# Two blocks on one core: the rotary rotation of the first two projections taken from TensorE and given to VectorE as four signed 32-row multiplications

## Chip, core and metric

One core of one Trainium2 chip runs the whole program as one launch. The metric is the device time in microseconds of that core, lower is better. The engines are named PE (TensorE), DVE (VectorE), ACT (ScalarE), POOL (GpSimd) and SP (SyncE, which issues DMAs).

## What is computed

The program is two layers of a first transformer (a sparse attention called NSA, then a dilated attention) and one layer of a second, on 512 tokens of width 1024. Each layer projects its normed input, turns queries and keys by a rotary embedding and attends. Only the rotary step matters here:

```python
def rope(x):
    T = x.shape[1]
    half = x.shape[-1] // 2
...
    x1, x2 = xf[..., :half], xf[..., half:]
    return jnp.concatenate([x1 * cos - x2 * sin, x2 * cos + x1 * sin], axis=-1).astype(x.dtype)
```

A head has 64 dimensions, so x1 and x2 are halves of 32. In the kernel a projected unit holds two heads on 128 rows (partitions), 512 tokens along a row: x1 and x2 of each head are quarters of 32 rows, and the rotation swaps neighbouring quarters and changes the sign of one.

## The kernel before

**A projection unit.** A projection is made in units of 128 output features by 512 tokens, each in one of four PSUM banks (unit u in bank u % 4). The weights of a unit are one piece of 512 KB. SP loads pieces into a ring of four slots (`ask_pieces`, L221). ACT copies the piece into a high part (`split_hi`, L232) and POOL subtracts to get the low part (`split_lo`, L240); three split pieces can be held. PE then makes 24 products of 128x512 for the unit (`feature_unit`, L264): 8 slices of the width by high-high, high-low, low-high. The first two or three units of a phase are interleaved in `feature_group` (L276).

**The rotary step** of unit r is `rope_parts`, in four instructions after ACT has copied the unit from PSUM to SBUF (L878 in the first projection, L1398 in the dilated one):
- PE multiplies the SBUF copy by a constant 128x128 matrix `rot` that swaps the quarters with sign, into bank 4 + r % 2 (L710, an fp32 product);
- POOL multiplies the SBUF copy by the cosine table into `t1` (L716);
- DVE multiplies the rotated PSUM bank by the sine table into `t2` in SBUF (L722);
- DVE adds `t1` and `t2` (L725), with both inputs in SBUF.

`t1` and `t2` have two buffers each, so the step of r waits for the sum of r-2 (semaphore `rope_roped`).

**First projection (NSA).** 23 units: two of the compression's input (u 0 and 1), ten that are turned (u 2 to 11, rotary r = u - 2), three pieces of the values (u 12 to 14), eight of the gate z. On PE, written out by hand: the units up to 11, the product of rotary step u - 4 behind unit u (r 0 to 7 so); then the compression's first layer, 8 unsplit pieces against taps of its input (L802, 64 matmuls, banks 6 and 7); then the products of r 8 and 9; then the values, where for each slice of the width four token tiles (i 0 to 3) are accumulated in banks 0 to 3 (`token_unit`, L305, 96 matmuls). The values' banks are those of units 8 to 11, so each tile first waits until ACT has evacuated that unit (`left2`). ACT's order is `split_hi` of u + 2, then the copy of u; its split of piece 12 stands ahead of its copy of unit 10. POOL's order is cosine of r 7, split of 12, cosine of r 8, split of 13, cosine of r 9, split of 14.

**Dilated projection.** 32 units (8 queries, 8 keys, 8 values, 8 z), of which 16 are turned: PE makes the product of r = u - 2 behind unit u, u 2 to 17. Values are transposed on PE behind units 17 to 24. ACT copies unit r into `raw6`, four buffers, and waits for the sum of r - 4.

The second transformer has five rotary steps of its own (`rope_two`), which use `rope_parts` with another table.

Of the kernel before, what the change touches and what calls it, by code (L numbers as in the profile page):

```python
# [24 lines left out]
ALU = mybir.AluOpType  # L25
# [3 lines left out]
P = 128  # L29
T = 512  # L30
# [4 lines left out]
HALF = DH // 2  # L35
# [67 lines left out]
V_COLS = 2 * P + 3 * NH  # L103
# [5 lines left out]
def build(nc, w_stream, consts_in, small_dram, x_in, pos_in, perm_in, u_in, v_in, u_rows, out, gates_dram, gelu_dram):  # L109
    ctx = ExitStack()  # L110
    with ctx:
# [3 lines left out]
        def sem(name):  # L115
            return ctx.enter_context(nc.semaphore(name))
# [32 lines left out]
        def C(name):  # L149
            a, b = CONST_AT[name]  # L150
            return cst[:, a:b]
# [191 lines left out]
        h_parts = (h_hi, h_lo)  # L343
# [356 lines left out]
        def rope_parts(tag, n, raw, t1, t2, dst, cos, sin, bank0, raw_ready):  # L700
# [25 lines left out]

            return pe_part, pool_part, dve_part, roped, sined

        def evacuated(order, sems):

            def wait(eng, i):
                sems[order[i]].wait(eng, sum(o == order[i] for o in order[:i + 1]))
            return wait
# [19 lines left out]
        ev2 = {who: since("evacuated_" + who, order2.count(who)) for who in ("dve", "act")}  # L753
        left2 = evacuated(order2, ev2)
        h1_sum, h1_done, cmp_sum, cmp_zero = sem("h1_sum"), sem("h1_done"), sem("cmp_sum"), sem("cmp_zero")
        rope_nsa = rope_parts("r0", 10, lambda r: rp[:, r, :], rt1, rt2, lambda r: qr[:, r, :],
                              C("cos"), C("sin"), 4, lambda eng, r: left2(eng, r + 2))
        sc = area(WORK, 2, NH * CMP_PAD)
        pc = area(WORK + 1272, 2, NH * CMP_PAD)
        ptc = area(WORK + 2296, 4 * P)  # L760
# [12 lines left out]
        with phase() as block:  # L773
# [5 lines left out]
            def _(pe):  # L779
                def free(u):  # L780
                    if u >= 4:
                        left2(pe, u - 4)

                feature_group(pe, units2[0:2], (0, 1), h_parts, n0.done)
                for u in range(2, 12):
                    free(u)
                    feature_unit(pe, piece_of(u), u % 4, h_parts)
                    if u >= 4:
                        rope_nsa[0](pe, u - 4)

                for kv in range(2):
                    if kv == 0:
                        left2(pe, 1)
                    for q4 in range(4):
                        w = piece_ready(pe, PIECES["cmp_w1"][kv * 4 + q4])
                        for m in range(4):
# [5 lines left out]
                                mm = pe.matmul(o, wt, x[:, kv, :, tap:tap + 8 * (N_CMP - 1) + 1:8],  # L802
                                               start=(tap == 0), stop=(tap == 15))
                        mm.then_inc(piece_used, 1)
                rope_nsa[0](pe, 8)
                rope_nsa[0](pe, 9)
                token_unit(pe, PIECES["vsw"], 0, V_COLS, 3, h_parts, tile_tokens,
                           lambda pe, i: left2(pe, 8 + i))
                pe.wait_ge(h1_done, 2)
                for g in range(2):  # L810
                    for ch in range(2):
# [37 lines left out]

                for u in range(15, 23):  # L850
                    if u < 17:
                        rope_nsa[4].wait(pe, u - 6)
                    else:
                        left2(pe, u - 2)
                    if u == 22:
                        pe.wait_ge(c_sub, TT)
                        ada_chunk(pe, 2, ada_sum2, 0)
                    feature_unit(pe, piece_of(u), 4 + (u - 15) % 2, h_parts)
                    if u == 16:
                        cmp_scores(0)  # L860
                        cmp_scores(1)
                        cmp_scores(2)
                    elif u == 17:
                        cmp_turn(0)
                        cmp_scores(3)
                    elif 18 <= u < 21:
                        cmp_turn(u - 17)
                        cmp_values(u - 18)
                    elif u == 21:
                        cmp_values(3)  # L870
# [437 lines left out]
        with phase() as block:  # L1308
# [19 lines left out]
            def act5(act):  # L1328
                for u in range(KD):
# [9 lines left out]
        vd = area(12288, TT, D)  # L1339
        od = area(16384, TT, D)  # L1340
        raw6 = area(16384, 4, T)
        rt61, rt62 = area(18432, 2, T), area(19456, 2, T)
        vt6 = area(20480, 2, T)
        v_turned, v_taken = sem("v_turned"), sem("v_taken")
        order6 = ["act"] * 32
        ev6 = {who: since("evacuated_" + who, order6.count(who)) for who in ("dve", "act")}
        left6 = evacuated(order6, ev6)
        rope_dil = rope_parts("r6", 16, lambda r: raw6[:, r % 4, :], rt61, rt62,
                              lambda r: (qd if r < 8 else kd)[:, r % 8, :], C("cos"), C("sin"), 4, left6)
        units6 = [n for name in ("dq", "dk", "dv", "dz") for n in PIECES[name]]  # L1350
        orders_in = sem("orders_in")
        orders = area(23552, 2 * P + 2 * TT + TT * NH)
        to_tile, to_class = orders[:, 0:P], orders[:, P:2 * P]
# [2 lines left out]
        with phase() as block:  # L1356
# [5 lines left out]
            @block.tensor  # L1362
            def _(pe):
                n1.pe_spread(pe)
                feature_group(pe, units6[0:3], (0, 1, 2), h_parts, n1.done)
                for u in range(2, 32):
                    if u >= 4:
                        left6(pe, u - 4)
                    if u >= 3:
                        feature_unit(pe, units6[u], u % 4, h_parts)  # L1370
                    if 2 <= u < 18:
                        rope_dil[0](pe, u - 2)
                    if 17 <= u < 25:
                        v = u - 17
                        left6(pe, u - 1)
                        if v >= 2:
                            pe.wait_ge(v_taken, v - 1)
                        for i in range(TT):
                            mm = pe.transpose(ps[:, 6 + v % 2, i * P:(i + 1) * P],
                                              vt6[:, v % 2, i * P:(i + 1) * P], ident)  # L1380
                        mm.then_inc(v_turned, 1)
# [1106 lines left out]
def constants():  # L2488
# [3 lines left out]
    def put(name, a):  # L2492
        lo, hi = CONST_AT[name]
        c[:, lo:hi] = a.reshape(P, hi - lo)
# [13 lines left out]
    inv = inv.astype(np.float32)[p % HALF]  # L2508
    angle = (np.arange(T, dtype=np.float32)[None, :] * inv[:, None]).astype(np.float64)
    put("cos", np.cos(angle))  # L2510
    put("sin", np.sin(angle))
    u = np.arange(T)
    put("causal", np.where(u[None, :] - (T - P) <= p[:, None], 0.0, -BIG))
    d = p[:, None] - p[None, :]
# [117 lines left out]
```

## Time and profile before

| | us |
|---|---|
| median of 3 runs | 2369.14 |
| lowest and highest of them | 2362.18, 2375.37 |
| the profiled execution, its time | 2366.45 |
| its span, first to last instruction | 2364.7 |
| PE busy in the span | 2251.7 |
| DVE, ACT, POOL busy | 1519.5, 917.4, 1313.3 |
| mean granted clock of PE | 0.975 of 2.4 GHz |

A trace is one execution. Time on it is counted from the first instruction. The first projection runs from about 52 to 220 us, the attention of NSA after it to about 445, the dilated projection from 508 to 703. A "wait" is the idle time of an engine ahead of an instruction and what ended it. "PEclk" is the clock that PE was granted: 1.00 is 2.4 GHz, 0.50 is 1.2 GHz. PE's durations overlap: the pitch of its instructions, start to start, is what they cost.

### The profile page before, as it was taken

Reading aid. Unit: us, or ns where it says so; the run is one execution under the profiler, and the core shown is the slowest. Engines: PE = TensorE matmul, PEld = TensorE weight load, DVE = VectorE, ACT = ScalarE, POOL = GpSimd, SP = SyncE. Lnnn points to the kernel's source line nnn. Section 1 sums busy time; section 2 is a strip of 40 time slices with the busy share of each in tenths; the row PEclk is TensorE's granted clock in tenths of the full one; section 3 lists DMA queues with packets and bytes.
Section 4 is the critical chain, followed back from the end, with each engine's and each line's share of the span. In section 5 each row is a group of like instructions: output and inputs, shape, how many; then the busy total and the mean of one; then the engine's idle time right before and its main releaser. Section 6 shows DMA issues by size and latency. Waiting matters only on the chain.

```text
span 2364.7 us, 31984 instructions
## 1 busy us (share of the span) xinstructions
PE 2251.7 (95%) x11853; PEld 1965.8 (83%) x11853; DVE 1519.5 (64%) x2899; ACT 917.4 (39%) x1513; POOL 1313.3 (56%) x691
## 2 busy tenths in 40 slices
PE   5999999889999889998999999999999999999999
PEld 4788787777778778777899999999999778777877
DVE  6526878544314533642299999999993666666765
ACT  2224555332237432533233333455554333333332
POOL 0532010236431234124268888766666999999996
PEclk9999999889999889998999999999999999999999
DMA  7243646322220212022158878899998999999996
GB/s 265 89 131 110 203 163 211 111 75 89 80 71 1 72 64 79 19 72 91 62 172 298 281 264 282 288 376 343 329 345 309 337 340 349 339 345 342 345 341 246
DMA packets 164474, 492.40 MB, mean 208 GB/s; under 512 B 15072, under 2 KB 64608, under 8 KB 162912
## 3 DMA queue, kind: packets, MB, share of 16 engines
q1 hardware_dynamic: 107872, 305.79, 37.6%
q0 software_dynamic: 36864, 134.23, 15.7%
q10 hardware_dynamic: 19584, 50.34, 5.6%
q8 instruction: 95, 1.56, 0.3%
q14 instruction: 59, 0.48, 0.1%
HBM read 437.87 MB, written 52.43 MB: 207 GB/s over the span
## 4 chain that ended last, share of the span: by engine, by line
POOL 21%; PE 15%; DVE 12%; issue 1%; DMA 1%; ACT 0%; DVEq 0%; ACTq 0%; POOLq 0%
POOL t_split L2239 13%; PE ps L2095 10%; POOL arena L2260 8%; PE ps L2113 4%; PE ps L2131 2%; DVE arena L2326 1%; DVE arena L2317 1%; DVE arena L2318 1%; DVE arena L2357 1%; DVE arena L2322 1%; DVE arena L2313 1%; DVE rope L2295 1%; DVE arena L2352 1%; DVE norm_rows L2295 1%; DVE arena L2295 1%
## 5 line engine op out<-in xcount | busy, mean ns | idle before, releaser
L2239 POOL TENSOR_TENSOR t_split<-t_raw,t_split 128x1024 fp32r<-128x1024 f32 x256 | 625.3, 2444 | 138.9 <-ACT t_split L2165 135.2
L240 POOL TENSOR_TENSOR w_split<-ring,w_split 128x1024 fp32r<-128x1024 f32 x113 | 273.2, 2421 | 508.9 <-ACT w_split L232 497.6
L2095 PE MATMUL ps<-h_hi,t_split 128*128 128x384 f32 x2048 | 537.0, 338 | 5.5 <-ACT e_gel L2171 3.0
L2131 PE MATMUL ps<-t_split,w_split 128*128 128x512 f32 x2304 | 531.5, 391 | 9.3 <-POOL t_split L2239 7.8
L2131 PEld LDWEIGHTS ps<-t_split,w_split 128*128 128x128 f32 x2304 | 429.7, 188 | 111.0 <-POOL t_split L2239 20.0
L264 PE MATMUL ps<-h_hi,w_split 128*128 128x512 f32 x1440 | 464.8, 398 | 0.0
L2165 ACT ACTIVATE t_split<-t_raw 128x1024 fp32r<-128x1024 f32 x256 | 270.7, 1058 | 359.9 <-DMA t_raw<-v_table 213.2
L2095 PEld LDWEIGHTS ps<-h_hi,t_split 128*128 128x128 f32 x2048 | 373.2, 189 | 7.9 <-POOL t_split L2239 4.4
L2095 PE MATMUL ps<-h_lo,t_split 128*128 128x384 f32 x1024 | 343.7, 336 | 0.0
L264 PEld LDWEIGHTS ps<-h_hi,w_split 128*128 128x128 f32 x1440 | 270.3, 188 | 61.7 <-issue 6.0
L264 PE MATMUL ps<-h_lo,w_split 128*128 128x512 f32 x720 | 280.6, 390 | 0.0
L232 ACT ACTIVATE w_split<-ring 128x1024 fp32r<-128x1024 f32 x113 | 119.1, 1058 | 366.3 <-PE ps L264 235.2
L2401 DVE TENSOR_TENSOR arena<-arena 128x1536 f32<-128x1536 f32 x32 | 118.5, 3703 | 178.2 <-DMA arena<-gates_scratch 178.2
L2260 POOL DMA_INDIRECT arena<-v_table,arena x128 | 199.6, 1559 | 20.8 <-issue 20.5
L2095 PEld LDWEIGHTS ps<-h_lo,t_split 128*128 128x128 f32 x1024 | 193.6, 189 | 0.0
L2171 ACT ACTIVATE e_gel<-ps 128x384 f32<-128x384 f32 x128 | 63.1, 493 | 320.7 <-PE ps L2095 264.5
L2418 DVE SCALAR_TENSOR_TENSOR ps<-arena,ps 128x1024 f32<-128x1024 f32 x127 | 162.9, 1283 | 14.6 <-DMA arena<-v_table,arena 7.9
L264 PEld LDWEIGHTS ps<-h_lo,w_split 128*128 128x128 f32 x720 | 135.2, 188 | 33.3 <-issue 6.0
L1123 PE MATMUL ps<-arena 128*128 128x64 f32 x916 | 133.7, 273 | 0.0
L2392 DVE TENSOR_SCALAR arena<-ps,arena 128x128 f32<-128x128 f32 x384 | 131.9, 419 | 0.0
L1219 POOL TENSOR_TENSOR arena<-arena,gtmp 128x512 f32<-128x512 f32 x16 | 20.3, 1270 | 200.3 <-DVE gtmp L1209 200.3
L1123 PEld LDWEIGHTS ps<-arena 128*128 128x128 f32 x916 | 127.9, 203 | 2.0
(316 smaller groups left out, 3219.2 us busy)
## 6 DMA issues: line engine op xcount, KB each, us to landing
ring<-w_stream SPq DMA_DIRECT2D x219, 512.0 KB, 3.3
t_raw<-u_table SPq DMA_DIRECT2D x128, 512.0 KB
t_raw<-v_table SPq DMA_DIRECT2D x128, 512.0 KB
gelu_scratch<-e_gel ACTq DMA_DIRECT2D x128, 192.0 KB
gates_scratch<-arena ACTq DMA_DIRECT2D x8, 3072.0 KB
arena<-gelu_scratch SPq DMA_DIRECT2D x32, 768.0 KB, 5.3
arena<-gates_scratch SPq DMA_DIRECT2D x32, 768.0 KB
xT<-x_in SPq DMA_DIRECT2D x2, 1024.0 KB, 11.3
```

The source lines that it names most:

```text
L232: act.activation(w_split[:, i % RS, 0, :], ring[:, n % R, :], ACT.Copy).then_inc(hi_done, 1)
L240: pool.tensor_tensor(w_split[:, i % RS, 1, :], ring[:, n % R, :], w_split[:, i % RS, 0, :].bitcast(F32), ALU.subtract).then_inc(lo_done, 1)
L264: mm = pe.matmul(ps[:, bank, :], w[:, a, k * P:(k + 1) * P], src[b][:, k, :], start=(k + a + b == 0), stop=(k == KD - 1 and a == 1))
L1123: mm = pe.matmul(ps[:, 5 + (m // 8) % 2, (m % 8) * DH:(m % 8 + 1) * DH], prt[:, m % TB, b * P:(b + 1) * P], v, start=(b == 0), stop=(b == ...
L2095: mm = pe.matmul(ps[:, 6 + n % 2, 0:NT], t_split[:, n % RAWS, u, k * P:(k + 1) * P], h_parts[h][:, k, P:T], start=(k + u + h == 0), stop=( ...
L2131: mm = pe.matmul(ps[:, 2 * i + half, :], w_split[:, b % 2, w, at:at + P], t_split[:, m % RAWS, v, half * 512:(half + 1) * 512], start=(n + ...
L2165: act.activation(t_split[:, m % RAWS, 0, :], t_raw[:, m % RAWS, :], ACT.Copy).then_inc(t_hi, 1)
L2239: pool.tensor_tensor(t_split[:, m % RAWS, 1, :], t_raw[:, m % RAWS, :], t_split[:, m % RAWS, 0, :].bitcast(F32), ALU.subtract).then_inc(t_ ...
L2260: pool.indirect_dma_start(out=vrows[j % NBV][:, :], out_offset=None, in_=v_in, in_offset=bass.IndirectOffsetOnAxis(ap=idx[:, j:j + 1], axis=0)
L2392: dve.tensor_scalar(hot_a[:, r * QT + s, :], ps[:, 3, 0:P], selT[:, 0, t + s:t + s + 1], selT[:, 2, t + s:t + s + 1], ALU.is_equal, ALU.mu ...
L2401: dve.tensor_tensor(gel, gel, gateb[:, s, :].rearrange("p (c e t) -> p e c t", e=VB, t=CHUNK), ALU.mult).then_inc(weighed, 1)
L2418: dve.scalar_tensor_tensor(out=acc, in0=vrows[j % NBV], scalar=w_tok[:, j:j + 1], in1=acc, op0=ALU.mult, op1=ALU.add).then_inc(v_added, 1)
```

## The change

`rope_direct` replaces `rope_parts` for the ten rotary steps of NSA and the sixteen of the dilated layer. It has no product. DVE reads the projected unit from its own PSUM bank, in four instructions of 32 rows each, multiplies by a sine table that carries the sign, and writes each quarter to its neighbour's rows of PSUM bank 4 + r % 2. The sum then takes `t1` from SBUF and the other operand from PSUM. The cosine stays on POOL and the copy to SBUF on ACT.

Because DVE now reads the unit's bank, PE may write that bank again only when both ACT's copy and the four sine instructions of its old unit are done. These waits stand ahead of each unit four later, and ahead of each token tile of the values.

```diff
+        def rope_direct(n, raw, t1, dst, bank, raw_ready):
+            cosed, sined, roped = since("rope_cosed", n), since("rope_sined", 4 * n), since("rope_roped", n)
+
+            def pool_part(pool, r):
+                raw_ready(pool, r)
+                if r >= 2:
+                    roped.wait(pool, r - 1)
+                pool.tensor_tensor(t1[:, r % 2, :], raw(r), C("cos"), ALU.mult).then_inc(cosed.sem, 1)
+
+            def dve_part(dve, r):
+                raw_ready(dve, r)
+                if r >= 2:
+                    roped.wait(dve, r - 1)
+                for at in range(0, P, HALF):
+                    to = at ^ HALF
+                    dve.tensor_tensor(ps[to:to + HALF, 4 + r % 2, :], ps[at:at + HALF, bank(r), :],
+                                      C("sin")[at:at + HALF, :], ALU.mult).then_inc(sined.sem, 1)
+                cosed.wait(dve, r + 1)
+                sined.wait(dve, 4 * (r + 1))
+                dve.tensor_tensor(dst(r), t1[:, r % 2, :], ps[:, 4 + r % 2, :], ALU.add).then_inc(roped.sem, 1)
+
+            def free(pe, r):
+                sined.wait(pe, 4 * (r + 1))
+
+            return free, pool_part, dve_part, roped
...
-        rope_nsa = rope_parts("r0", 10, lambda r: rp[:, r, :], rt1, rt2, lambda r: qr[:, r, :],
-                              C("cos"), C("sin"), 4, lambda eng, r: left2(eng, r + 2))
+        rope_nsa = rope_direct(10, lambda r: rp[:, r, :], rt1, lambda r: qr[:, r, :], lambda r: (r + 2) % 4,
+                               lambda eng, r: left2(eng, r + 2))
...
                 def free(u):
                     if u >= 4:
                         left2(pe, u - 4)
+                    if u >= 6:
+                        rope_nsa[0](pe, u - 6)
...
                     feature_unit(pe, piece_of(u), u % 4, h_parts)
-                    if u >= 4:
-                        rope_nsa[0](pe, u - 4)
...
-                rope_nsa[0](pe, 8)
-                rope_nsa[0](pe, 9)
-                token_unit(pe, PIECES["vsw"], 0, V_COLS, 3, h_parts, tile_tokens,
-                           lambda pe, i: left2(pe, 8 + i))
+                def free_for_values(pe, i):
+                    left2(pe, 8 + i)
+                    rope_nsa[0](pe, 6 + i)
+
+                token_unit(pe, PIECES["vsw"], 0, V_COLS, 3, h_parts, tile_tokens, free_for_values)
...
-                        rope_nsa[4].wait(pe, u - 6)
+                        rope_nsa[3].wait(pe, u - 6)
...
+        rope_dil = rope_direct(16, lambda r: raw6[:, r % 4, :], rt61, lambda r: (qd if r < 8 else kd)[:, r % 8, :],
+                               lambda r: r % 4, left6)
...
                     if u >= 4:
                         left6(pe, u - 4)
+                    if 4 <= u < 20:
+                        rope_dil[0](pe, u - 4)
                     if u >= 3:
                         feature_unit(pe, units6[u], u % 4, h_parts)
-                    if 2 <= u < 18:
-                        rope_dil[0](pe, u - 2)
...
-    put("sin", np.sin(angle))
+    put("sin", np.where(np.arange(P)[:, None] % (2 * HALF) < HALF, 1.0, -1.0) * np.sin(angle))
```

The order of PE where the compression ends and the values begin, before (`ps` is PSUM, `w_split` the split weights, `h_hi` and `h_lo` the parts of the input, in brackets the semaphores waited for):

```order
L802 MATMUL ps<-arena,ring 128x62 [waits piece_in3]
L802 MATMUL ps<-arena,ring 128x62 x7
L710 MATMUL ps<-arena,cst 128x512 [waits rope_sined,evacuated_act] x2
L305 MATMUL ps<-w_split,h_hi 128x304 [waits evacuated_act,lo_done]
L305 MATMUL ps<-w_split,h_lo 128x304
L305 MATMUL ps<-w_split,h_hi 128x304
L305 MATMUL ps<-w_split,h_hi 128x304 [waits evacuated_act]
```

And the same place of the changed kernel, with PE's line numbers of its own:

```order
L830 MATMUL ps<-arena,ring 128x62 [waits piece_in3]
L830 MATMUL ps<-arena,ring 128x62 x7
L305 MATMUL ps<-w_split,h_hi 128x304 [waits rope_sined,evacuated_act,lo_done]
L305 MATMUL ps<-w_split,h_lo 128x304
L305 MATMUL ps<-w_split,h_hi 128x304
L305 MATMUL ps<-w_split,h_hi 128x304 [waits rope_sined,evacuated_act]
```

The two rotary products between the compression and the values are gone, and each of the four token tiles now waits for a rotary step's sine as well.

On DVE, one rotary step of the first projection before:

```order
L722 TENSOR_TENSOR arena<-ps,cst 128x512 [waits rope_roped,rope_rotated]
L725 TENSOR_TENSOR arena<-arena 128x512 [waits rope_sined,rope_cosed]
L969 COPY arena<-ps 64x31 [waits cmp_zero,cmp_sum]
```

And in the changed kernel:

```order
L746 TENSOR_TENSOR ps<-ps,cst 32x512 [waits rope_roped,evacuated_act]
L746 TENSOR_TENSOR ps<-ps,cst 32x512 x3
L750 TENSOR_TENSOR arena<-arena,ps 128x512 [waits rope_sined,rope_cosed]
L998 COPY arena<-ps 64x31 [waits cmp_zero,cmp_sum]
```

Two instructions of a step have become five, and the first waits for ACT's copy where it waited for PE's product.

## Rows read from the trace of the kernel before

**Rows 1.** The page, busy time of each engine, whole span.
```profile
PE 2251.7 (95%) x11853; PEld 1965.8 (83%) x11853; DVE 1519.5 (64%) x2899; ACT 917.4 (39%) x1513; POOL 1313.3 (56%) x691
```

**Rows 2.** Stretches of the trace (us, busy by engine, granted clock, DMA share, GB/s).
```profile
60.00:126.00 66.00, 66.00 (x278) 51.89 (x277) 31.22 (x27) 13.55 (x17) 34.58 (x18) 1.00 0.24 80
158.00:220.00 62.00, 62.00 (x333) 53.08 (x333) 34.85 (x47) 22.58 (x31) 16.14 (x7) 1.00 0.37 128
527.00:625.00 98.00, 98.00 (x404) 75.20 (x403) 47.40 (x32) 24.77 (x32) 59.08 (x32) 1.00 0.26 90
```

**Rows 3.** Timeline of ACT (start us, us, engine, line, operation, idle before), 75 to 88 us.
```profile
75.95 0.60 ACT L878 ACTIVATE arena<-ps 128x512 f32<-128x512 f32 x1 [3.89 <-PE ps L264]
81.39 0.60 ACT L878 ACTIVATE arena<-ps 128x512 f32<-128x512 f32 x1 [3.89 <-PE ps L264]
87.74 0.60 ACT L878 ACTIVATE arena<-ps 128x512 f32<-128x512 f32 x1 [4.80 <-PE ps L264]
```

**Rows 4.** The product's line L710, 60 to 150 and 500 to 640 us (ns min/median/max).
```profile
L710 PE MATMUL ps<-arena,cst x20: 590/591/697, 81.2 to 144.2; 128*128 128x512 f32 x20
...
L710 PE MATMUL ps<-arena,cst x32: 590/590/591, 527.1 to 622.8; 128*128 128x512 f32 x32
```

**Rows 5.** Timelines of DVE, POOL and ACT around one rotary unit of the dilated projection.
```profile
547.22 0.69 DVE L722 TENSOR_TENSOR arena<-ps,cst 128x512 f32<-128x512 f32 x1 [3.06 <-PE ps L710]
548.02 2.48 DVE L725 TENSOR_TENSOR arena<-arena 128x512 f32<-128x512 f32 x1
...
547.56 2.40 POOL L240 TENSOR_TENSOR w_split<-ring,w_split 128x1024 fp32r<-128x1024 f32 x1 [1.96 <-ACT w_split L232]
550.65 1.29 POOL L716 TENSOR_TENSOR arena<-arena,cst 128x512 f32<-128x512 f32 x1 [0.69 <-DVE arena L725]
...
546.42 1.06 ACT L232 ACTIVATE w_split<-ring 128x1024 fp32r<-128x1024 f32 x1 [4.80 <-PE ps L264]
```

**Rows 6.** Timelines of PE, DVE, POOL and ACT, 140 to 150 us.
```profile
142.01 1.13 PE L710 MATMUL ps<-arena,cst 128*128 128x512 f32 x2 [0.66 <-ACT arena L878]
...
145.71 0.44 PE L305 MATMUL ps<-w_split,h_hi 128*128 128x304 f32 x2
...
143.17 0.69 DVE L722 TENSOR_TENSOR arena<-ps,cst 128x512 f32<-128x512 f32 x1 [15.00 <-PE ps L710]
...
141.54 2.35 POOL L240 TENSOR_TENSOR w_split<-ring,w_split 128x1024 fp32r<-128x1024 f32 x1 [24.63 <-ACT w_split L232]
143.85 1.28 POOL L716 TENSOR_TENSOR arena<-arena,cst 128x512 f32<-128x512 f32 x1
...
141.37 0.58 ACT L878 ACTIVATE arena<-ps 128x512 f32<-128x512 f32 x1
```

**Rows 7.** DVE timeline from 49 us: alternating full-width operations, then four half-width copies.
```profile
51.69 0.74 DVE L582 SCALAR_TENSOR_TENSOR arena<-xT,amp,ps 128x512 f32<-128x512 f32 x1
52.35 0.74 DVE L587 SCALAR_TENSOR_TENSOR h_lo<-arena,mod,h_hi 128x512 fp32r<-128x512 f32 x1
...
62.35 1.78 DVE L951 COPY arena<-ps 64x256 f32<-64x256 f32 x4 [1.77 <-PE ps L276]
...
L951 DVE COPY arena<-ps x8: 416/422/428, 62.4 to 70.7; 64x256 f32<-64x256 f32 x8
```

**Rows 8.** Line L2418, a sum of an SBUF and a PSUM operand, 1800 to 1900 us.
```profile
L2418 DVE SCALAR_TENSOR_TENSOR ps<-arena,ps x19: 1275/1287/1292, 1828.7 to 1895.6; 128x1024 f32<-128x1024 f32 x19
...
1800.00:1900.00 100.00, 96.75 (x439) 80.10 (x437) 57.57 (x33) 34.18 (x33) 86.64 (x46) 1.00 0.94 341
```

**Rows 9.** Stretches around two idle times of PE, then a fall of its clock.
```profile
220.00:221.00 1.00, 1.00 (x5) 0.56 (x3) 0.00 (x0) 0.00 (x0) 0.00 (x0) 1.00 0.00 0
221.00:224.00 3.00, 0.07 (x1) 0.00 (x0) 1.45 (x1) 2.59 (x3) 1.98 (x2) 0.90 0.01 3
...
1380.00:1383.00 3.00, 0.02 (x2) 0.04 (x1) 2.86 (x9) 2.24 (x4) 0.00 (x0) 1.00 0.74 261
1384.00:1387.00 3.00, 3.00 (x11) 3.00 (x10) 2.96 (x2) 1.12 (x2) 2.99 (x1) 0.50 0.27 97
```

More of the change, by code:

```diff
@@ L1341, in build @@
         raw6 = area(16384, 4, T)
-        rt61, rt62 = area(18432, 2, T), area(19456, 2, T)
+        rt61 = area(18432, 2, T)
         vt6 = area(20480, 2, T)
@@ L1347, in build @@
         left6 = evacuated(order6, ev6)
-        rope_dil = rope_parts("r6", 16, lambda r: raw6[:, r % 4, :], rt61, rt62,
-                              lambda r: (qd if r < 8 else kd)[:, r % 8, :], C("cos"), C("sin"), 4, left6)
         units6 = [n for name in ("dq", "dk", "dv", "dz") for n in PIECES[name]]
+        rope_dil = rope_direct(16, lambda r: raw6[:, r % 4, :], rt61, lambda r: (qd if r < 8 else kd)[:, r % 8, :],
+                               lambda r: r % 4, left6)
         orders_in = sem("orders_in")
```

## The prediction

> **What bounds the kernel now.** I read the busy shares of the engines first: PE is busy 2251.7 of 2364.7 us [rows 1]. A mean over stages proves nothing, so next the two stages of the change. From 60 to 126 and from 527 to 625 us PE is busy in every microsecond at full clock, while DVE is busy about half the time, POOL 52% and 60%, and DMA a quarter [rows 2]. So is PE from 158 to 220 us, behind the place where the first ten rotary steps end: time that PE saves there is not lost in a wait further on. The later phases start when the one ahead ends, so I let a shift pass through to the end.
>
> Then the pace. ACT copies each unit right after PE ends it, so the starts of its copies show PE's pitch. Without a rotary product between them it is 81.39 - 75.95 = 5.44 us, with one 87.74 - 81.39 = 6.35 us [rows 3]. **A product costs PE 0.91 us.** Its own two passes of 590 ns each [rows 4] overlap their neighbours, so the pitch is what counts. There are 26 of them: 52 records, two to a product [rows 4].
>
> **What goes.** Eight products stand behind units of the first projection and sixteen behind units of the dilated one. 24 x 0.91 = 21.8 us leave PE. Is PE then paced by something else, at 5.44 us a unit? Feeding: POOL splits a piece in 2.40 us and makes a cosine in 1.29 [rows 5], 3.7 us of 5.44. ACT begins the split of piece u + 3 when PE has ended unit u, takes 1.06 us, and POOL is done 3.6 us after that end (546.42 - 0.1 to 547.56 + 2.40) [rows 5]; PE wants the piece two units, 10.9 us, after it. Cover of 7 us is left. A piece of 512 KB per 5.44 us is 96 GB/s, where the stretches now move 80 and 90 [rows 2] and a later stage 341 [rows 8].
>
> **What DVE gets.** A step was one sine (0.69 us) and one sum that took 2.48 us [rows 5], since it ran beside POOL's work and both its inputs were in SBUF. It becomes four sines of 32 rows and a sum with one input in PSUM.
> - A sine: time goes by columns, not rows. 64x256 copies take 0.42 us and 128x512 work 0.69 [rows 6, 7], so 32x512 should take 0.69. No row shows DVE multiplying from PSUM into PSUM over other rows; the nearest below is 0.69, above it twice the time per column (0.27 us per 256 columns more, so 1.23). I take 0.69, since 1024-column work that reads and writes PSUM takes 1.28 [rows 8], 0.27 per 256 columns as elsewhere.
> - Their pitch: alternating full-width instructions start 0.66 us apart at 0.74 each, overlapped by 0.08; the four copies that go to alternating halves of the rows take 1.78 us in all, a pitch of 0.45 at 0.42, not overlapped [rows 7]. The sines alternate in the same way. I take 0.69 + 0.03 = 0.72, so 2.86 us for four. The Trainium skill (VectorE: DVE Perf Modes, section on two Vector instructions with no wait between them) says that an instruction that starts in another 32-row group than the last one's is held until the earlier ones have finished. The copies agree. Overlapped as the others are, four would take 2.5 us, and the stall below would be 0.3 us shorter.
> - The sum: 19 instructions like it, with one SBUF and one PSUM input, stay between 1.275 and 1.292 us while POOL is busy 87% of the time [rows 8]. A 0.69 us sine of before lay within POOL's 141.54 to 143.89 us as well [rows 6]. So 0.69, where it was 2.48.
>
> A step on DVE is then about 2.86 + 0.1 + 0.69 = 3.65 us of 5.44. The reuse of a bank is free too: the sines of a unit start at most 1.8 us after PE has ended it and finish by 4.7, POOL's cosine is ready at about 5.0, and PE wants the bank three units, 16 us, later. In both unit loops I cost DVE at nothing, covered by PE.
>
> **Where it shows.** The values. Their token tiles want the banks of units 8 to 11, and the change adds the wait for rotary steps 6 to 9. On the clock of before: PE ended the compression at 142.01 - 0.66 = 141.35 [rows 6]. ACT copied unit 10 by 141.95 and POOL had piece 12 split at 143.89, the cosine of step 8 at 145.13 [rows 6]; all these hang on PE's use of the ring, and so shift with it. DVE makes the sines of step 8 from 142.0 to 144.9, waits for the cosine, adds from 145.2 to 145.9, and only then makes the sines of step 9: 145.9 + 2.9 = 148.8. PE starts tiles 0 to 2 at 143.9, idles from about 145.3, and starts tile 3 at 148.8. Before, tile 3 was the tenth matmul at 145.71 + 0.14 = 145.85 [rows 6]. **The stall costs 2.95 us**, with the two removed products already counted in it. What is queued behind it on PE is the whole rest.
>
> PE then has idled 2.6 us, worked 1.3, and idled 3.5. After 3.3 us of idle at 221 us the clock fell to 0.50, the level of 1.2 GHz, and after 3.0 us at 1380 too [rows 9]. The work after it ran about 5.7 us at half clock in the first case and 3.2 in the second; half of each is lost, 2.85 and 1.6 us. **I take 2.2 us for the clock.** The Trainium skill (TensorE: Matmul & The Clock Gate, section on HAM oscillation) has the rule that idle gaps of PE bring the throttle back and work must release it; the trace agrees, and without this cost the sum would be 2.2 us more of gain.
>
> **Sum.** 21.8 - 2.95 - 2.2 = 16.6 us. 2366.45 - 16.6 = 2349.8 us. The profiled execution lies 2.7 us below the median of the three runs, 2369.14, and within their span; I keep its time as the base. About 0.5%, 12 us, is what a measurement of this kernel can tell from no change.
>
> **Rivals.**
> 1. *All the gain arrives.* The values' stall is covered or the clock doesn't fall, and falls elsewhere cost a little less. For: the granted clock's mean is 0.975, so falls are worth tens of microseconds in all and hang on chance. Against: the order on POOL and DVE gives the stall without any luck. All 26 products gone is 23.7 us: 2342.8. Without the clock alone it is 2347.6. Chance 0.15.
> 2. *Sines into PSUM at half speed*, 1.23 us. A step on DVE is then 5.8 us, over 5.44, but the lag of 0.4 us a unit fits the three units of slack (16 x 0.4 = 6.4 of some 9). The stall grows to about 7 us, since both sets of sines lie on it: 21.8 - 7 - 2.2 = 12.6, so 2353.8. Against: [rows 8]. Chance 0.08.
> 3. *Something else paces the units*, or the change just moves PE's time into waits: a piece that comes late, ACT's copy behind a split, a clock that gives back twice what I took. Gain 0 to 9 us, 2357 to 2366, taken as 2362. Against: the 7 us of cover above. That the change doesn't do what it says would show the same: products that cost PE nothing. The two pitches of [rows 3] speak against that. Chance 0.12.
> 4. *Slower: DVE becomes the bound.* Each sine reads its table from SBUF. If these reads were kept out by POOL as the old sum was (2.48 for 0.69 [rows 5]), a step would take POOL's 3.7 us plus DVE's own 3.6, 7.3 us. The group of three units ended at 527.1 [rows 4], so unit 0's copy at about 523.5 (5.4 us before, and 1.8 for ACT). Sixteen steps from there end at 640. Before, PE began the unit that will want the last bank some 7 us behind the last product at 622.8 [rows 4], at 630. That is 10 us late; with the first projection's stall of 3.5 and some lag and clock, about 15 us slower, 2381. It decides from 6.65 us a step, (630 - 523.5) / 16. The 0.69 us sine under POOL's split [rows 6] speaks against it, one case only. Chance 0.04.
>
> **Numbers.** The forecast, 2345 to 2354 with the bounds of the stall and the clock, has 0.61. The low end of the range is rival 1 in full; the high end takes in rival 2 and most of rival 3. Left out are rival 4, the rest of 3 and runs that lie as high as the highest of before. Faster by over 0.5% is the forecast, most of rival 1 and 2, less what scatter takes: 0.78. Within 0.5%: rival 3 and that scatter, 0.17. Slower: rival 4 and little else, 0.05.
>
> **What would show it.** Right: copies of ACT 5.44 us apart throughout both unit loops; DVE's sines at 0.69 us, four in 2.9, and sums at 0.69 beside POOL; PE idle of about 3.5 us ahead of the values' fourth tile with "DVE ps" as what ended it, and a stretch at half clock behind it; the dilated projection 14.6 us shorter. Wrong: sines of 1.2 us, or stretched to POOL's ends; PE waits inside the unit loops; the dilated projection shorter by much less than 14 us.

## The result and the profile after

| | before | changed |
|---|---|---|
| median of 11 runs, us | 2368.24 | 2350.63 |
| lowest and highest | 2362.18, 2375.37 | 2344.94, 2360.64 |
| ratio, 95% interval | | 0.9928 [0.9913, 0.9943] |
| the profiled execution, time and span | 2366.45, 2364.7 | 2357.37, 2355.6 |

Faster by 17 us (0.7%, 13 to 21 by the interval), where 16.6 us was forecast. The profiled execution of the changed kernel is one of its slower ones; why its span shows only 9 us is told below. Of all executions in this document one, of e4, took 4574.11 us and is left out of its ratio as slow.

The page of the changed kernel, span and busy times:

```profile
span 2355.6 us, 31939 instructions
...
PE 2238.0 (95%) x11801; PEld 1963.8 (83%) x11801; DVE 1530.1 (65%) x2977; ACT 914.9 (39%) x1513; POOL 1307.7 (56%) x691
```

PE's busy time fell by 13.7 us against [rows 1], DVE's rose by 10.6 us only, though it has 78 instructions more: most sums became cheaper, for two reasons that are told apart below.

Stretches of the changed kernel (columns as in [rows 2]), the unit loop of the first projection, then its last token tiles and gate units:

```profile
60.00:120.00 60.00, 60.00 (x268) 49.71 (x267) 38.86 (x54) 13.99 (x18) 34.38 (x18) 1.00 0.27 88
152.00:215.00 63.00, 63.00 (x348) 54.40 (x347) 31.34 (x47) 23.62 (x32) 17.78 (x7) 1.00 0.41 134
```

PE is still busy in every microsecond of both, DVE in 65% of the first instead of 47%. The pace is in ACT's copies of neighbouring units:

```profile
98.14 0.60 ACT L907 ACTIVATE arena<-ps 128x512 f32<-128x512 f32 x1 [3.89 <-PE ps L264]
103.58 0.60 ACT L907 ACTIVATE arena<-ps 128x512 f32<-128x512 f32 x1 [3.89 <-PE ps L264]
```

They start 5.44 us apart, the pitch that units without a product had before [rows 3]; the units with one stood 6.35 us apart. The new sines (L746) and sums (L750) on DVE, all of them:

```profile
L746 DVE TENSOR_TENSOR ps<-ps,cst x104: 690/700/709, 73.0 to 606.2; 32x512 f32<-32x512 f32 x104
...
L750 DVE TENSOR_TENSOR arena<-arena,ps x26: 686/689/689, 76.5 to 607.3; 128x512 f32<-128x512 f32 x26
```

And one step of the dilated projection, DVE first, then POOL:

```profile
565.95 2.89 DVE L746 TENSOR_TENSOR ps<-ps,cst 32x512 f32<-32x512 f32 x4 [1.50 <-ACT arena L1427]
569.19 0.69 DVE L750 TENSOR_TENSOR arena<-arena,ps 128x512 f32<-128x512 f32 x1 [0.35 <-POOL arena L738]
...
565.51 2.40 POOL L240 TENSOR_TENSOR w_split<-ring,w_split 128x1024 fp32r<-128x1024 f32 x1 [1.79 <-ACT w_split L232]
567.88 1.29 POOL L738 TENSOR_TENSOR arena<-arena,cst 128x512 f32<-128x512 f32 x1
```

Four sines take 2.89 us, a pitch of (2.89 - 0.70) / 3 = 0.73 us, while POOL splits a piece beside them. The sum takes 0.69 us, where it took 2.48 beside POOL's split [rows 5]. It waits 0.35 us for the cosine, which costs nothing: the next unit's copy comes later still.

This sum has no split of POOL beside it: it starts when the cosine is done, and POOL's next split begins only at 570.95. So it is with 21 of the 26 sums. And with POOL idle the old sum took 0.69 us too, with both inputs in SBUF:

```profile
127.47 0.69 DVE L725 TENSOR_TENSOR arena<-arena 128x512 f32<-128x512 f32 x1
```

For these 21 the new place in time is enough to explain the shorter sum. The other five lie wholly within a split of POOL, two of them at the values (one is shown below) and three at the start of the dilated projection, and they take 686 to 689 ns as well. Of the rotary sums only those five show that one with an operand in PSUM isn't held up; the like sums of [rows 8] agree.

The dilated projection, its group of three units (L276) and its other units (L264), first and last start on PE:

```profile
L276 PE MATMUL ps<-h_hi,w_split x48: 389/389/794, 513.2 to 531.2; 128*128 128x512 f32 x48
...
L264 PE MATMUL ps<-h_hi,w_split x468: 388/389/481, 499.8 to 692.9; 128*128 128x512 f32 x156
```

From 513.2 to 692.9 it takes 179.7 us. In the trace of the kernel before the same two lines ran from 508.2 to 703.0, 194.8 us: 15.1 us less.

The place where the compression (now L830) ends and the values (L305) begin, PE, then DVE, then POOL:

```profile
119.70 14.86 PE L830 MATMUL ps<-arena,ring 128*128 128x62 f32 x128
...
137.17 0.41 PE L305 MATMUL ps<-w_split,h_hi 128*128 128x304 f32 x1 [2.60 <-POOL w_split L240]
...
138.85 0.46 PE L305 MATMUL ps<-w_split,h_hi 128*128 128x304 f32 x1
142.15 0.59 PE L305 MATMUL ps<-w_split,h_hi 128*128 128x304 f32 x1 [2.85 <-DVE ps L746]
...
135.20 2.90 DVE L746 TENSOR_TENSOR ps<-ps,cst 32x512 f32<-32x512 f32 x4 [21.87 <-ACT arena L907]
138.40 0.69 DVE L750 TENSOR_TENSOR arena<-arena,ps 128x512 f32<-128x512 f32 x1 [0.30 <-POOL arena L738]
139.12 2.89 DVE L746 TENSOR_TENSOR ps<-ps,cst 32x512 f32<-32x512 f32 x4
...
134.76 2.35 POOL L240 TENSOR_TENSOR w_split<-ring,w_split 128x1024 fp32r<-128x1024 f32 x1 [23.77 <-ACT w_split L232]
137.06 1.30 POOL L738 TENSOR_TENSOR arena<-arena,cst 128x512 f32<-128x512 f32 x1
138.31 2.36 POOL L240 TENSOR_TENSOR w_split<-ring,w_split 128x1024 fp32r<-128x1024 f32 x1
```

This answers to [rows 6]. PE waits 2.60 us for the split of piece 12, works on three tiles, and waits 2.85 us for DVE, which could begin step 9's sines only behind the sum of step 8, and that only behind POOL's cosine. That sum, 138.40 to 139.09, lies within POOL's split of 138.31 to 140.67. The fourth tile starts at 142.15, 22.45 us behind the first matmul of the compression. Before it started 145.85 - 126.48 = 19.37 us behind it. **The stall costs 3.1 us.** The granted clock there (last three figures of a row: clock, DMA share, GB/s):

```profile
139.00:142.00 3.00, 0.31 (x2) 0.00 (x0) 2.88 (x5) 0.33 (x1) 3.00 (x3) 0.50 0.47 158
142.00:145.00 3.00, 2.85 (x11) 2.88 (x12) 0.70 (x2) 0.00 (x0) 2.22 (x1) 0.50 0.38 147
145.00:146.00 1.00, 1.00 (x9) 1.00 (x8) 0.00 (x0) 0.00 (x0) 0.00 (x0) 0.94 0.65 152
```

The clock fell at about 138.3, 1.1 us behind the first wait and ahead of the second (from 138 to 139 its mean is 0.65). Behind the second wait PE works at 1.2 GHz until shortly after 145.0. From the fourth tile to the first gate unit it takes 157.1 - 142.15 = 14.95 us, where it took 159.4 - 145.85 = 13.55 before: 1.4 us for the clock.

One table holds what the rest rests on. "Values" is the time on PE from the compression's first matmul to the first of the gate units, "dilated" that from the first to the last unit of that projection, "attention" that from the last gate unit to the first unit of NSA's output projection, which the change doesn't touch. All from the starts of those lines in one trace each, read to 0.1 us, so that a difference of 0.1 says nothing.

| kernel | values, us | half clock in it | attention | dilated |
|---|---|---|---|---|
| before | 32.9 | no | 232.1 | 194.8 |
| changed | 37.4 | yes | 237.8 | 179.7 |
| changed, again (e8) | 37.5 | yes | 234.7 | 179.8 |
| copies first (e1) | 35.1 | yes | 232.0 | 180.0 |
| first projection only (e2) | 37.5 | yes | 231.5 | 194.8 |
| dilated only (e3) | 33.0 | no | 232.7 | 179.9 |
| before, copies first (e4) | 31.9 | no | 232.8 | 194.1 |
| gap filled (e5) | 32.4 | no | 228.2 | 179.5 |
| sines together (e6) | 37.0 | yes | 229.3 | 180.4 |
| sines twice (e7) | 37.4 | yes | 232.4 | 194.1 |

The attention's column is the largest part of the scatter between these traces: the same work takes 228 to 238 us, with the granted clock of a trace's 215 to 500 us at 0.90 in the changed kernel's profile and 0.93 in that of the kernel before. That trace of the changed kernel has the longest one, and lost 5.7 us there. Another 1.6 us were lost from the output projection to the dilated one, and 1.7 ahead of the first projection and behind the dilated one together: 18.1 gained and 9.0 lost, the 9 us of the spans. Sums are therefore tested on stages, not on totals.

### The profile page after: what moved, and what is told of

Same layout as the page of the kernel before. It is cut to its first block, busy times and chain, and to the rows that moved or that the text cites. A ratio compares the mean times of both kernels' runs of the same rounds, so it can differ in the third digit from the quotient of the medians.

```text
span 2355.6 us, 31939 instructions
## 1 busy us (share of the span) xinstructions
PE 2238.0 (95%) x11801; PEld 1963.8 (83%) x11801; DVE 1530.1 (65%) x2977; ACT 914.9 (39%) x1513; POOL 1307.7 (56%) x691
## 4 chain that ended last, share of the span: by engine, by line
POOL 19%; PE 16%; DVE 12%; DMA 2%; issue 1%; ACT 0%; DVEq 0%; ACTq 0%; POOLq 0%
POOL t_split L2268 12%; PE ps L2124 10%; POOL arena L2289 7%; PE ps L2142 4%; PE ps L2160 2%; DMA t_raw<-v_table 2%; DVE arena L2355 1%; DVE arena L2346 1%; DVE arena L2347 1%; DVE arena L2386 1%; DVE arena L2351 1%; DVE arena L2342 1%; DVE rope L2324 1%; DVE arena L2381 1%; DVE norm_rows L2324 1%
## 5 line engine op out<-in xcount | busy, mean ns | idle before, releaser
L264 PE MATMUL ps<-h_hi,w_split 128*128 128x512 f32 x1440 | 451.7, 392 | 0.0
L264 PEld LDWEIGHTS ps<-h_hi,w_split 128*128 128x128 f32 x1440 | 270.4, 188 | 56.5 <-issue 0.7
L264 PE MATMUL ps<-h_lo,w_split 128*128 128x512 f32 x720 | 280.2, 389 | 0.0
L2430 DVE TENSOR_TENSOR arena<-arena 128x1536 f32<-128x1536 f32 x32 | 108.5, 3389 | 168.5 <-DMA arena<-gates_scratch 168.4
L2289 POOL DMA_INDIRECT arena<-v_table,arena x128 | 193.6, 1512 | 20.7 <-issue 20.0
L2447 DVE SCALAR_TENSOR_TENSOR ps<-arena,ps 128x1024 f32<-128x1024 f32 x127 | 163.0, 1283 | 15.1 <-DMA arena<-v_table,arena 8.6
L264 PEld LDWEIGHTS ps<-h_lo,w_split 128*128 128x128 f32 x720 | 135.2, 188 | 28.4 <-issue 0.7
```

Source lines behind the costliest of these rows:

```text
L264: mm = pe.matmul(ps[:, bank, :], w[:, a, k * P:(k + 1) * P], src[b][:, k, :], start=(k + a + b == 0), stop=(k == KD - 1 and a == 1))
L2289: pool.indirect_dma_start(out=vrows[j % NBV][:, :], out_offset=None, in_=v_in, in_offset=bass.IndirectOffsetOnAxis(ap=idx[:, j:j + 1], axis=0)
L2430: dve.tensor_tensor(gel, gel, gateb[:, s, :].rearrange("p (c e t) -> p e c t", e=VB, t=CHUNK), ALU.mult).then_inc(weighed, 1)
L2447: dve.scalar_tensor_tensor(out=acc, in0=vrows[j % NBV], scalar=w_tok[:, j:j + 1], in1=acc, op0=ALU.mult, op1=ALU.add).then_inc(v_added, 1)
```

## Experiments

Ratios are to the kernel before, run beside each kernel. The first four ran on one chip, the last four on another.

**e1: the stall's cause.** ACT and POOL in another order:

```diff
                 for u in range(1, 12):
-                    split_hi(act, piece_of(u + 2))
+                    if u < 10:
+                        split_hi(act, piece_of(u + 2))
                     if u >= 2:
                         unit(u)
+                split_hi(act, piece_of(12))
+                split_hi(act, piece_of(13))
...
-                    if 12 <= u < 15:
-                        rope_nsa[1](pool, u - 5)
+                    if u == 12:
+                        for r in (7, 8, 9):
+                            rope_nsa[1](pool, r)
```

> The changed kernel, but ACT copies units 10 and 11 ahead of its splits of pieces 12 and 13, and POOL makes the cosines of steps 8 and 9 ahead of its split of piece 12. Theory (the stall ahead of the fourth token tile comes from the order on ACT, POOL and DVE, and costs 3.3 us of idle time plus a fall of PE's clock): the sines of steps 8 and 9 are done while the compression runs, PE waits before the values only for the split of piece 12 (2.6 us), the stretch from the end of the compression to the first gate unit takes 17 to 18 us instead of 22.5, and the kernel gains 4 to 5 us on the changed one, about 2346, ratio to before about 0.991. Rival (the fall of the clock is there anyway, because of the 2.6 us): the stretch takes 19.5 to 20.5 us, a gain of 2 to 3 us. Rival (DVE or the bank is the limit, not the order): the stretch stays at 22 us.

2342.39 us, ratio 0.9881 [0.9861, 0.9900]. Its timelines of PE and DVE, and three stretches:

```profile
120.62 11.20 PE L830 MATMUL ps<-arena,ring 128*128 128x62 f32 x96
132.27 6.00 PE L830 MATMUL ps<-arena,ring 128*128 128x62 f32 x32 [0.45 <-DMA ring<-w_stream]
138.29 0.62 PE L305 MATMUL ps<-w_split,h_hi 128*128 128x304 f32 x1
...
121.44 2.89 DVE L746 TENSOR_TENSOR ps<-ps,cst 32x512 f32<-32x512 f32 x4 [1.76 <-ACT arena L907]
...
131.00:133.00 2.00, 1.55 (x14) 1.35 (x13) 0.00 (x0) 0.00 (x0) 0.00 (x0) 1.00 0.94 334
133.00:134.00 1.00, 1.00 (x9) 1.00 (x9) 0.00 (x0) 0.00 (x0) 0.00 (x0) 0.74 0.93 328
134.00:143.00 9.00, 8.97 (x39) 8.79 (x39) 0.00 (x0) 4.78 (x6) 7.02 (x3) 0.50 0.68 250
```

Step 9's sines start at 121.44, and PE goes from the compression to the values without waiting for DVE: the stall was the order's. From the compression's first matmul the stretch takes 35.1 us, 2.3 less than in the changed kernel, the amount of the first rival. The number that the expectation named, from the end of the compression to the gate units, is 155.7 - 138.3 = 17.4 us, and would fit the theory's 17 to 18; but it does so only because the compression itself took 17.65 us instead of 14.86 and ended later. The theory had no fall of the clock, and there was one, so it is the first rival's gain that came, though not by its way: the clock did not fall at the values. It fell at about 133.5 us (a mean of 0.74 from 133 to 134), **while PE was busy**, in the compression's products of 62 columns, 1.2 us behind a wait of 0.45 us for a piece: the last fourth of them took 6.00 us where the first three took 11.20. The total says more than 2.3 us: its interval lies below the changed kernel's 0.9913 to 0.9943, but touches that of the same kernel in e8, 0.9897 to 0.9936. Where a rest would come from, the trace doesn't show.

**e2 and e3: each projection alone.** The other one gets its products back, with a matrix in place of `rot` that swaps the quarters too but whose entries are -1 wherever they aren't zero, since the table now has the sign. e2, at the dilated projection (e3 does the same to the first):

```diff
-        rope_dil = rope_direct(16, lambda r: raw6[:, r % 4, :], rt61, lambda r: (qd if r < 8 else kd)[:, r % 8, :],
-                               lambda r: r % 4, left6)
+        rope_dil = rope_parts("r6", 16, lambda r: raw6[:, r % 4, :], rt61, rt62,
+                              lambda r: (qd if r < 8 else kd)[:, r % 8, :], C("cos"), C("sin"), 4, left6, "rotm")
...
-                    if 4 <= u < 20:
-                        rope_dil[0](pe, u - 4)
...
+                    if 2 <= u < 18:
+                        rope_dil[0](pe, u - 2)
```

> The new rotary step in the first projection alone; the dilated one makes its 16 products again (by a matrix whose entries are all -1, since the sine table now carries the sign). Theory: the first projection gives 8 x 0.91 = 7.3 us in its units and loses 4.5 to 5 us ahead of and in the values, so 2 to 3 us of gain on the kernel before, 2366, ratio 0.999. Rival (the scatter of the total hides a larger share): 7 us or more of gain.

2364.71 us, ratio 0.9973 [0.9961, 0.9986]: 3 to 9 us. In the trace the first projection, from its first matmul to its last gate unit, takes 219.1 - 52.7 = 166.4 us against 220.7 - 51.8 = 168.9: 2.5 us, as the theory had it; the total shows some more, which the trace doesn't place. The rival's 7 us lie within the interval of the total, so it is the stage alone that speaks against it. The dilated projection is that of before:

```profile
L276 PE MATMUL ps<-h_hi,w_split x48: 387/389/796, 506.0 to 524.8; 128*128 128x512 f32 x48
...
L264 PE MATMUL ps<-h_hi,w_split x464: 387/389/799, 525.4 to 700.8; 128*128 128x512 f32 x155
```

> The new rotary step in the dilated projection alone; the first one makes its ten products again. Theory: PE's pitch there falls from 6.35 to 5.44 us for 16 units, 14.5 us of gain, no wait of PE within the units, 2354, ratio 0.994. Rival (DVE's longer step or the feeding of pieces paces the units): a pitch above 5.6 us and less than 11 us of gain.

2352.82 us, ratio 0.9935 [0.9914, 0.9955], 15 us, and its dilated projection:

```profile
L276 PE MATMUL ps<-h_hi,w_split x48: 389/389/796, 507.6 to 525.9; 128*128 128x512 f32 x48
...
L264 PE MATMUL ps<-h_hi,w_split x464: 388/389/481, 526.1 to 687.5; 128*128 128x512 f32 x155
```

From 507.6 to 687.5, 179.9 us, 14.9 less than before; the first projection's values take 33.0 us, before 32.9, with no fall of the clock. So some 15 us of the gain come from the dilated layer and 2.3 to 2.9 from the first (the traces of e8, e2 and the changed kernel), which gives most of its 7.3 us back.

**e4: the same order in the kernel before.** The change of e1 made to `before`.

> The kernel before, with the same new order on ACT and POOL as the first of these runs. Theory: only the two short waits of PE for ACT's copies ahead of the products of steps 8 and 9 go, 1.2 us, of which the split of piece 12 (ready 2.5 us after the compression, while two products take some 1.8) takes about half back: 0 to 1 us of gain, ratio 0.999 to 1.000. Rival (the new order is worth the same in both kernels): 4 us or more.

2365.33 us as the median of all 12 executions, 2363.54 without the one of 4574 us, ratio 0.9971 [0.9954, 0.9989]; the values' stretch 31.9 us against 32.9. The stage agrees with the theory (1.0 us). The total shows more than the stage, 2.6 to 11 us by its interval: of the 11 executions that count, five took 2367 to 2373 us and six 2356 to 2364. The one with a trace is of the upper group, so where the lower group gained is open, and a few microseconds of a total can't be put down to the new order.

**e5: is the clock the idle time's?** e1 and two products that nobody reads (the wait is for the sum of step 8, the last to read bank 4):

```diff
+                rope_nsa[3].wait(pe, 9)
+                for i in range(2):
+                    pe.matmul(ps[:, 4, :], ident, C("cos"), start=True, stop=True)
+
                 def free_for_values(pe, i):
```

> The first of these runs (copies and cosines first), and two fp32 products of 128x512 that nobody reads on PE between the compression and the values, into bank 4. Theory (idle time of PE there, behind the light products of the compression, brings the clock down; three of three kernels without the two products of steps 8 and 9 showed a fall there, none of the three with them): the two fit into the 2.6 us of waiting, the clock stays at 2.4 GHz, and from the first matmul of the compression to the first of the gate units it takes 32 to 33 us, against 35.1 in the first run. Rival (the compression's narrow products bring the fall by themselves): 34 to 36 us, with half clock in it, and a total no different from the first run's.

2343.33 us, ratio 0.9897 [0.9875, 0.9919]. PE's timeline and two stretches:

```profile
119.03 14.86 PE L830 MATMUL ps<-arena,ring 128*128 128x62 f32 x128
133.71 1.90 PE L835 MATMUL ps<-cst 128*128 128x512 f32 x4
136.53 0.41 PE L305 MATMUL ps<-w_split,h_hi 128*128 128x304 f32 x1 [0.92 <-POOL w_split L240]
...
133.00:137.00 4.00, 3.08 (x15) 1.77 (x14) 0.00 (x0) 3.15 (x3) 2.88 (x2) 1.00 0.81 254
137.00:145.00 8.00, 8.00 (x60) 8.00 (x59) 0.00 (x0) 2.68 (x5) 6.16 (x3) 1.00 0.72 222
```

The products fit into the wait, of which 0.92 us is left, and the clock stays at 2.4 GHz: 32.4 us, the theory's number, 5.1 less than the changed kernel on the same chip. Over all traces: six of six without products between compression and values have half clock there, four of four with them have none. That the filling is what held the clock is likely by this, not more: in e1 it fell ahead of the place where the gap would be filled, so idle time there isn't all, and one trace of e5 doesn't exclude a fall in other executions. Nor is it the length of the wait: in e2, e7 and e8 the clock was down 0.7 to 0.9 us behind the last narrow product, with most of the wait still to come (e8's rows are below). What the narrow products and the gap each have in it stays open.

**e6: the order on DVE.** The sines of steps 8 and 9 first, then their sums:

```diff
-                for r in range(10):
-                    rope_nsa[2](dve, r)
+                for r in range(8):
+                    rope_nsa[2](dve, r)
+                for part in (4, 5):
+                    rope_nsa[part](dve, 8)
+                    rope_nsa[part](dve, 9)
```

> The changed kernel, but DVE makes the sines of step 9 ahead of the sum of step 8, which waits for POOL's cosine. Theory: step 9's sines start right behind step 8's and end 1.0 us earlier (0.3 of waiting and 0.7 of the sum), so PE's idle time ahead of the fourth token tile is 1.8 us instead of 2.85; the total moves less than its scatter. Rival (the wait is for ACT's copy of unit 11 or for POOL): it stays at 2.8 us.

One run, 2346.57 us. DVE, then PE's fourth tile:

```profile
135.21 5.82 DVE L746 TENSOR_TENSOR ps<-ps,cst 32x512 f32<-32x512 f32 x8 [21.19 <-ACT arena L913]
141.06 0.69 DVE L752 TENSOR_TENSOR arena<-arena,ps 128x512 f32<-128x512 f32 x1
...
141.17 0.59 PE L305 MATMUL ps<-w_split,h_hi 128*128 128x304 f32 x1 [1.35 <-DVE ps L746]
```

Eight sines run through in 5.82 us, and the wait is 1.35 us. Counted from the compression's first matmul (120.4) the tile starts at 20.8 us where it started at 22.45: 1.6 earlier, of which 1.0 is the order, as expected, and the rest that the splits and copies ahead of it came earlier in this execution. The clock fell all the same and the stretch takes 37.0 us: a shorter stall alone bought little in this one execution.

**e7: how long a step DVE can hide.** In the dilated projection the four sines twice (with a wait of the second four for the first one of the first four):

```diff
-                for at in range(0, P, HALF):
+                for i, at in enumerate(list(range(0, P, HALF)) * again):
+                    if i == 4:
+                        sined.wait(dve, 4 * again * r + 4)
```

> The changed kernel with each of the four sines of the dilated projection made twice: a step of DVE of about 6.7 us instead of 3.7. Theory (DVE's step is hidden up to about 5.7 us, and 6.65 us gives the whole gain of this stage back): 16 steps take 107 us, PE waits for DVE's sines some 14 us in all, and the stage goes from 180 to about 194 us, total 2363 to 2367. Rival (DVE is hidden at any such length, or only the pace of its last steps counts): less than 5 us more.

2363.80 us, ratio 0.9983 [0.9967, 0.9998], 17 us above the changed kernel beside it. DVE, PE's waits ahead of units, and the units' first and last start:

```profile
601.24 5.82 DVE L748 TENSOR_TENSOR ps<-ps,cst 32x512 f32<-32x512 f32 x8
607.16 0.69 DVE L752 TENSOR_TENSOR arena<-arena,ps 128x512 f32<-128x512 f32 x1
...
607.16 0.47 PE L264 MATMUL ps<-h_hi,w_split 128*128 128x512 f32 x1 [0.92 <-issue]
613.80 0.47 PE L264 MATMUL ps<-h_hi,w_split 128*128 128x512 f32 x1 [0.94 <-issue]
...
L264 PE MATMUL ps<-h_hi,w_split x464: 387/389/481, 525.1 to 700.6; 128*128 128x512 f32 x155
```

PE's units stand 613.80 - 607.16 = 6.64 us apart, as DVE's steps do, and each waits for its eighth sine, here until 601.24 + 5.82 = 607.06 ("issue" in the trace, since the wait is for several semaphores). The first units still ran at 5.44; then the three banks of lead were used up. The stage takes 194.1 us, as expected, and nearly the whole gain of the dilated layer is gone. The slower rival was reckoned to decide from 6.65 us a step; the stage stands at that point, 0.7 us below the 194.8 of before.

**e8: the changed kernel again.**

> The changed kernel unaltered, on the same chip as the runs beside it. Theory: 17 us below the kernel before, ratio 0.993; the fall of the clock at the values again; the stretch from the compression to the gate units 37 us again; and 3 to 8 us above the run with the filled gap. Rival (the first profile's fall was chance): no half clock there and a stretch of 35 us.

2347.08 us, ratio 0.9916 [0.9897, 0.9936]. The compression, the waits of PE ahead of the first and fourth tile, and the clock:

```profile
120.09 14.86 PE L830 MATMUL ps<-arena,ring 128*128 128x62 f32 x128
...
137.26 0.62 PE L305 MATMUL ps<-w_split,h_hi 128*128 128x304 f32 x1 [2.31 <-POOL w_split L240]
142.23 0.59 PE L305 MATMUL ps<-w_split,h_hi 128*128 128x304 f32 x1 [2.32 <-DVE ps L746]
...
135.00:136.00 1.00, 0.00 (x0) 0.00 (x0) 0.69 (x1) 0.61 (x2) 1.00 (x1) 0.92 0.86 307
136.00:138.00 2.00, 0.74 (x3) 0.74 (x4) 1.92 (x3) 1.98 (x3) 2.00 (x2) 0.50 0.86 277
138.00:143.00 5.00, 2.68 (x11) 2.33 (x11) 4.37 (x7) 1.88 (x4) 5.00 (x4) 0.50 0.64 204
143.00:146.00 3.00, 3.00 (x14) 3.00 (x13) 0.00 (x0) 0.00 (x0) 1.31 (x1) 0.50 0.33 108
```

The same two waits, half clock again, and 37.5 us. The fall is earlier here: the mean of 0.92 from 135 to 136 puts it at about 135.8, 0.9 us behind the compression's end and ahead of the first tile. This kernel lies 3.8 us above e5 in the medians of the same chip; the intervals overlap, so it is the stage, not the total, that shows the 5.1 us.

## Why the prediction was right, point by point

- **PE is the bound and a product costs its pitch.** Forecast 5.44 us a unit, measured 5.44; 14.6 us in the dilated projection, measured 15.1 (14.9 in e3). Right.
- **DVE's instructions.** Sine 0.69, measured 0.70; four 2.86, measured 2.89; sum 0.69, measured 0.689. The sum came out as forecast partly for another reason than the one given: 21 of the 26 ran with POOL idle, where the old one took 0.69 as well; the five within a split bear the reason out. One reading in the working is off: from 0.69 to 1.28 us for 512 more columns is 0.30 per 256 columns, not 0.27, which changes nothing in the sum. The two bounds of the sine lay at 0.69 and 1.23: the lower held, and rival 2 is out. The pitch of 0.73 at 0.70 is that of instructions that wait for their forerunner, not the 0.66 at 0.74 of [rows 7]; the rule of the Trainium skill on changing start rows (VectorE: DVE Perf Modes, section on two Vector instructions with no wait between them) agrees with it.
- **Rival 4, DVE behind POOL.** No sine of 104 took over 0.709 us, though 51 of them lay wholly within a split of POOL. Out; e7, at 6.64 us a step, ends 0.7 us short of the stage before, which fits the threshold of 6.65.
- **Feeding, rival 3.** No wait of PE within either unit loop. Out.
- **The stall.** 2.95 us forecast, 3.1 measured, and e1 shows that it comes from the order on ACT, POOL and DVE. The idle time ahead of the fourth tile was 2.85 us, not the 3.5 of the forecast, since the three tiles ahead of it took 2.14 us instead of 1.3, a part of them at half clock.
- **The clock.** It fell as forecast, but 2.2 us was too much: 1.4 us in the first profile, and in e8 157.6 - 142.23 - 13.55 = 1.8. The term "the work after it ran about 5.7 us at half clock in the first case and 3.2 in the second; half of each is lost" left out that the fall comes before the second wait, so part of the half-clock time is idle: the clock was down from about 138.3 to 145.1, but behind the wait PE worked only the last 2.9 us of it, and half of that is the 1.4 us. The 1.0 us ahead of the wait cost nothing, since the wait was for DVE. The stall and the clock together were 5.15 us in the sum and 4.5 in the trace.
- **The sum.** The first projection gained 168.9 - 165.9, to the hundredth 2.93 us (2.1 forecast; 2.3 in e8), the dilated one 15.1: 18.1 by stages, 17 by the runs, 16.6 forecast. With an interval of 13 to 21 us on the runs, that the total agrees within half a microsecond is luck; it is the stages that bear the terms out.
- **Not foreseen:** the prediction gave the scatter of totals (12 us, measured 13 and 16 from lowest to highest), but not that NSA's attention has the largest part in it, nor that a new order and the filled gap (e5) bring nearly what rival 1, "all the gain arrives", would have: 7.5 us in the first projection and 15.3 in the dilated one, 22.8 of its 23.7. In the changed kernel itself that rival did not come true.

## What to carry to other kernels

Where PE is busy in every microsecond, price a small product at the change in the pitch of its neighbours, and pay for it with the engine whose step is still shorter than PE's pitch; that step costs nothing while it is shorter (3.65 us of 5.44 here), and when it is longer the lead of banks covers it only for the first few units (e7: 6.64 us a step took the gain back; lengths between weren't tried). When a consumer is added to a buffer, look for the one place where the lead is zero (here the first tiles of the values), because there the order on three other engines comes to light, with PE's clock in its wake. Put copies that free a bank ahead of splits that wait for a DMA.

## What the runs showed of the hardware beyond that

- An operand in PSUM takes a DVE sum out of the way of POOL's subtraction: it took 2.48 us beside it with both inputs in SBUF [rows 5], and 0.69 with one of them in PSUM, in all five sums of the changed kernel that lay wholly within such a subtraction.
- DVE multiplies 32 rows and writes them to other rows of PSUM in the time that 128 rows took from PSUM to the same rows of SBUF: 690 to 709 ns for 512 columns, where the old sine took 676 to 695.
- PE's clock fell to 1.2 GHz while PE was busy in every microsecond of the rows, on fp32 products of 62 columns (e1, at 133.5 us, 1.2 us behind a gap of 0.45 us). A busy PE in the rows is no promise of the full clock.
